# Readout: the projection of tile j ahead of the logits of tile j-2 in the tensor engine's turn

## The chip, the cores and the metric

The kernel runs on one NeuronCore of a Trainium2 chip. The core has five engines that run side by side, each with its own queue of instructions in program order: TensorE (PE, with its weight loads shown apart as PEld), VectorE (DVE), ScalarE (ACT), GpSimd (POOL) and SyncE (SP), which here issues DMAs. They meet at semaphores. The metric is the device time of one execution in microseconds (us), less is better; a figure for a kernel is the median of several runs.

## The reference

One layer of a diffusion backbone over 2048 latent tokens of width 1024, with 256 context tokens ahead of them. Two recurrent mixers (HGRN2 and RWKV-7) run in both directions, their outputs are normed and gated, projected and added to the residual, and a mixture of 64 experts in 8 groups follows, of which each token takes two. What the change touches is the end of the mixer and the routing:

```python
def token_mixer(...):
    ...
    out_l = jnp.concatenate([hgrn2_readout(o_l, g_l, hg_norm_w),
                             rwkv7_readout(y_l, *aux_l, rw_r_k, rw_gn_w, rw_gn_b)], -1) @ w_out
    ...
def hier_moe(h, ...):
    ...
    gl = (t @ w_group + b_group).astype(jnp.float32)
    g_idx = jnp.argmax(gl, -1)
    ...
    el = (t @ w_router).reshape(n_tok, N_GROUPS, EXPERTS_PER_GROUP) + b_router
    ...
    top_v, top_i = lax.top_k(el, TOP_K_INNER)
    ...
def reference(...):
    ...
        x = ln_affine(DN_ALPHA * x + g1 * y, ln1_g[l], ln1_b[l])
        h2 = layer_norm(x) * (1.0 + sc2) + sh2
```

## The kernel before

The program runs six stages one after the other: the two input projections, the scans, the readout, the experts and the combination. All engines meet at a barrier between stages. The change is in the readout (lines 1959 to 2455), which handles the 2048 tokens in 16 tiles of 128.

Each engine runs the same loop of turns, j from -1 to 18 (`readout_turns`, L2340), and in turn j it works on tiles at different depths. The order in a turn is written out by hand for each engine, and nothing but semaphores ties the engines' turns together.

For one tile i the work goes like this. DVE makes the right half of `mix` (turn i-1: `mean`, `variance`, `rw_gate`, L2138 to L2161, signals `mixed`), and POOL the left half (`hg_gate`, L2094, waits for `mixed`, signals `hg_part`). In turn i, PE turns mix into PSUM with eight transposes (`turn_mix`, L2293, all transposes are recorded at L2290), ACT copies them to SBUF as `mixT` (`mix_copy`, L2117), and PE multiplies them with `w_out` (`project`, L2324, matmuls at L2332: 16 in the program, two records each in the trace). In turn i+1 DVE adds the residual (`residual`, L2193, two instructions), takes moments, norms (L2203, L2204, and L2211, L2212, which make `h` and signal `h_ready`). SP stores h. In turn i+2 PE turns h (`turn_h`, L2300), ACT copies it to `hT` (`h_copy`, L2124), and PE makes the 72 router logits of the tile (`logits`, L2306, matmuls at L2314: 8 in the program, 16 records).

Four tiles make a batch b for the routing, which DVE does in four steps spread over four turns: `route_group`, `route_experts`, `route_onehot`, `route_rank`. `routed(j, step)` (L2346) gives the turn: step s of batch b is in turn 4b+5+s, for the last batch in turns 17 and 18. In DVE's turn the routing step stands behind the second moments (up to L2185) and ahead of `rw_gate` and `second_norm`. `pe_ranks` (L2321, L2322) is PE's part of the third step.

The waits around the change are these:

```python
def project(self, pe, i):
    pe.wait_ge(s["mix_copied"], 2 * i + 2)
    wait(pe, s["residual"], i)
...
def logits(self, pe, i):
    pe.wait_ge(s["h_copied"], 2 * i + 2)
    ...
    wait(pe, s["logits_read"], i // BATCH)
...
def h_copy(self, act, i):
    act.wait_ge(s["h_turned"], i + 1)
    wait(act, s["logits_done"], i)
...
def residual(self, dve, i):
    dve.wait_ge(s["projected"], i + 1)
...
def route_group(self, dve, b):
    dve.wait_ge(s["logits_done"], BATCH * (b + 1))
```

`project` and `residual` share one pair of PSUM buffers, so project(j) waits until residual(j-1) has read them. The first instruction of `route_group` behind its wait is L2230, which reads the logits of four tiles from PSUM.

Of the kernel before, what the change touches and what calls it, by code (L numbers as in the profile page):

```python
# [2339 lines left out]
def readout_turns(turn):  # L2340

    for j in range(-1, N_TILES + 3):
        turn(j, j % 2)


def routed(j, step):  # L2346

    for b in range(N_TILES // BATCH):
        last = b == N_TILES // BATCH - 1
        if j == BATCH * b + 5 + (step // 3 if last else step):  # L2350
            return b
    return None


def readout(nc, A, S, K):
    with ExitStack() as ctx:
        m = Mem(nc, ctx, "read")
        r = Readout(nc, m, A, S, K)
        s = r.s
        tile = lambda i: 0 <= i < N_TILES  # L2360

        with nc.Block() as block:
            @block.sync
            def _(sp):
                r.start_loads(sp)

                def turn(j, u):
                    if tile(j + 2) and not (isinstance(j, int) and j < 0):
                        r.load(sp, j + 2, u)
                    if tile(j):  # L2370
                        r.load_x(sp, j)
                    if tile(j - 1):
                        r.store(sp, j - 1)
                readout_turns(turn)
                sp.wait_ge(s["h_stored"], 16 * N_TILES)

            @block.gpsimd
            def _(pool):
                r.op = Order(pool, s["order_pool"])
                nc.gpsimd.memset(r.heps[:], HEAD_EPS).then_inc(s["eps_set"], 1)  # L2380
                nc.gpsimd.memset(r.yeps[:], GN_EPS).then_inc(s["eps_set"], 1)
                pool.wait_ge(s["eps_set"], 2)

                def turn(j, u):
                    if tile(j + 1):
                        r.hg_add(pool, j + 1, 1 - u)
                    if tile(j - 1):
                        r.power(pool, j - 1, 0)
                    if tile(j + 1):
                        r.hg_power(pool, j + 1)  # L2390
                        r.rw_power(pool, j + 1)
                    if tile(j - 1):
                        r.power(pool, j - 1, 1)
                    if tile(j + 1):
                        r.hg_gate(pool, j + 1, 1 - u)
                readout_turns(turn)

            @block.scalar
            def _(act):
                def turn(j, u):  # L2400
                    if tile(j):
                        r.mix_copy(act, j)
                    if tile(j - 2):
                        r.h_copy(act, j - 2)
                    if tile(j + 1):
                        r.hg_squares(act, j + 1, 1 - u)
                        r.y_square(act, j + 1)
                        r.v_scale(act, j + 1, 1 - u)
                        r.hg_scale(act, j + 1, 1 - u)
                    if routed(j, 2) is not None:  # L2410
                        r.exps(act, routed(j, 2))
                readout_turns(turn)

            @block.tensor
            def _(pe):
                def turn(j, u):
                    if tile(j):
                        r.turn_mix(pe, j)
                    if tile(j - 2):
                        r.turn_h(pe, j - 2)  # L2420
                    if routed(j, 3) is not None:
                        r.pe_ranks(pe, routed(j, 3))
                    if tile(j - 2):
                        r.logits(pe, j - 2)
                    if tile(j):
                        r.project(pe, j)
                readout_turns(turn)

            @block.vector
            def _(dve):  # L2430
                r.oa, r.ob, r.oc = (Order(dve, s[f"order_{x}"]) for x in "abc")
                nc.vector.memset(r.run[:], 0.0).then_inc(s["order_start"], 1)
                parts = (r.route_group, r.route_experts, r.route_onehot, r.route_rank)

                def turn(j, u):
                    if tile(j - 1):
                        r.residual(dve, j - 1)
                    if tile(j + 1):
                        r.mean(dve, j + 1, 1 - u)
                    if tile(j - 1):  # L2440
                        r.first_norm(dve, j - 1)
                    if tile(j + 1):
                        r.variance(dve, j + 1, 1 - u)
                    if tile(j - 1):
                        r.moments(j - 1, 1)
                    for step in range(4):
                        if routed(j, step) is not None:
                            parts[step](dve, routed(j, step))
                    if tile(j + 1):
                        r.rw_gate(dve, j + 1, 1 - u)  # L2450
                    if j == -1:
                        r.fold(dve)
                    if tile(j - 1):
                        r.second_norm(dve, j - 1)
                readout_turns(turn)
# [610 lines left out]
```

## Time and profile before

| | |
|---|---|
| median of three runs | 4197.87 us (4196.18 to 4203.44) |
| the profiled execution, whole | 4199.46 us |
| its span, first to last instruction | 4197.8 us |
| PE busy in the span | 3892.4 us, 93% |
| DVE busy in the span | 2049.4 us, 49% |
| ACT, POOL busy in the span | 1174.2 us and 1172.4 us, 28% each |
| the readout | from about 2396 to 2775 us of the span |

Busy time is the time in which an engine executes. An idle time is put down to whatever ended it, so "idle 2.46 <- PE" at an instruction of DVE means that DVE had nothing to do for 2.46 us until PE signalled. The granted clock of TensorE is given as a share of 2.4 GHz; 0.50 is 1.2 GHz. The ends of matmuls are modelled, so consecutive rows of PE can overlap a little.

### The profile page before, as it was taken

The numbers are of one execution on the slowest core, as the hardware profiler recorded it, in microseconds if no ns is written. First come the engines' busy times: TensorE is split into PE (matmuls) and PEld (weight loads), VectorE is DVE, ScalarE is ACT, GpSimd is POOL, SyncE is SP. The second block draws the span as 40 slices with busy tenths as digits, with TensorE's granted clock in tenths as the row PEclk, the third lists the DMA queues.
The fourth block names the chain that finished last, engine by engine and source line by source line (L and its number), as shares of the span: only waits on it lengthen the run. The fifth ranks groups of instructions, "written<-read, shape, count | busy, mean of one in ns | idle before, by whom it ended". The sixth has DMA issues, their size and how long they took to land. (4 is left out here: it accounts for less than half of the span.)

```text
span 4197.8 us, 102804 instructions
## 1 busy us (share of the span) xinstructions
PE 3892.4 (93%) x40204; PEld 2601.7 (62%) x40204; DVE 2049.4 (49%) x3485; ACT 1174.2 (28%) x2889; POOL 1172.4 (28%) x1498
## 2 busy tenths in 40 slices
PE   7999889999996999999999689859999999999988
PEld 5888666666666899999999645443333434343333
DVE  2221277677764776766766489951111111111116
ACT  1111244454543544544554333300000000000000
POOL 0000111101110545555654444433222222222220
PEclk9999899999998999999999889959999999999999
DMA  9821366656655444444444364434668999999986
GB/s 363 211 74 64 104 213 205 206 182 200 211 170 166 136 124 131 131 126 132 129 134 123 108 171 139 130 125 183 258 247 344 394 403 395 400 405 420 420 334 245
DMA packets 318478, 908.16 MB, mean 216 GB/s; under 512 B 67353, under 2 KB 164921, under 8 KB 269361
## 3 DMA queue, kind: packets, MB, share of 16 engines
q1 hardware_dynamic: 261056, 754.99, 51.1%
q0 software_dynamic: 46992, 131.41, 8.5%
q10 hardware_dynamic: 10080, 16.79, 1.1%
q8 instruction: 257, 4.21, 0.4%
q14 instruction: 93, 0.75, 0.1%
HBM read 960.84 MB, written 200.17 MB: 277 GB/s over the span
## 5 line engine op out<-in xcount | busy, mean ns | idle before, releaser
L2804 PE MATMUL exp_gate_up<-exp_w_gate,exp_rows_and_rowsT 128*64 128x512 f32 x1664 | 731.5, 596 | 13.4 <-DMA exp_w_up<-in_moe_w_up_dram 12.2
L2804 PE MATMUL exp_gate_up<-exp_w_up,exp_rows_and_rowsT 128*64 128x512 f32 x1664 | 732.0, 596 | 0.0
L2804 PEld LDWEIGHTS exp_gate_up<-exp_w_gate,exp_rows_and_rowsT 128*64 128x64 f32 x1664 | 227.7, 138 | 482.4 <-issue 482.4
L2755 DVE TENSOR_TENSOR exp_hidden<-exp_hidden,exp_gate_up 64x512 f32<-64x512 f32 x104 | 71.9, 692 | 701.0 <-ACT exp_hidden L2736 701.0
L884 PE MATMUL rwp_product<-rwp_hT,rwp_w_rw 128*128 128x256 f32 x1808 | 393.4, 380 | 12.2 <-DVEq L818 12.2
L1065 PE MATMUL hgp_product<-hgp_hT,const_w_hg 128*128 128x256 f32 x1664 | 379.0, 383 | 8.7 <-DVEq L1046 8.7
L2829 PE MATMUL exp_down<-exp_w_down,exp_hiddenT 128*64 128x512 f32 x1664 | 380.0, 597 | 3.2 <-issue 0.7
L884 PEld LDWEIGHTS rwp_product<-rwp_hT,rwp_w_rw 128*128 128x128 f32 x1808 | 343.9, 191 | 59.2 <-issue 12.6
L1065 PEld LDWEIGHTS hgp_product<-hgp_hT,const_w_hg 128*128 128x128 f32 x1664 | 313.8, 192 | 60.4 <-issue 10.8
L2736 ACT ACTIVATE exp_hidden<-exp_gate_up 64x512 f32<-64x512 f32 x104 | 61.2, 589 | 945.4 <-PE exp_gate_up L2804 945.4
L2713 POOL DMA_INDIRECT s_yb<-exp_out,exp_row_slot x104 | 104.4, 1004 | 571.8 <-PE exp_rows_turned L2789 446.5
L2332 PE MATMUL read_projected<-read_w_out,read_mixT 128*128 128x512 f32 x512 | 236.6, 622 | 8.6 <-DVE read_w_out L2173 7.2
L508 POOL TENSOR_TENSOR hg_scaled_qk<-hg_qkf,hg_exponent 128x256 f32<-128x256 f32 x224 | 199.7, 892 | 151.5 <-ACT hg_exponent L468 123.5
L1062 PE MATMUL hgp_product<-const_w_hg,hgp_hT 128*128 128x512 f32 x544 | 238.6, 594 | 2.4 <-DVEq L1046 2.4
L2829 PEld LDWEIGHTS exp_down<-exp_w_down,exp_hiddenT 128*64 128x64 f32 x1664 | 123.0, 136 | 185.5 <-issue 180.6
L2804 PEld LDWEIGHTS exp_gate_up<-exp_w_up,exp_rows_and_rowsT 128*64 128x64 f32 x1664 | 227.7, 138 | 0.0
L2767 DVE TENSOR_TENSOR exp_out<-exp_down,exp_out_gate 128x512 f32<-128x512 f32 x104 | 71.9, 692 | 305.5 <-PE exp_down L2829 305.5
L1686 PE MATMUL rw_inverse_bank<-rw_inverse_turned,rw_A_rho_beta 64*64 64x64 f32 x5760 | 194.4, 221 | 13.5 <-issue 8.5
L1694 PE MATMUL rw_inverse_bank<-rw_inverse,rw_X 64*64 64x64 f32 x5760 | 193.2, 220 | 3.5 <-ACT rw_X L1747 3.2
L581 DVE TENSOR_TENSOR hg_exponent<-hg_logf_sum 128x512 f32<-128x512 f32 x224 | 196.3, 876 | 0.0
L1686 PEld LDWEIGHTS rw_inverse_bank<-rw_inverse_turned,rw_A_rho_beta 64*64 64x64 f32 x5760 | 180.0, 136 | 23.8 <-issue 19.2
L1694 PEld LDWEIGHTS rw_inverse_bank<-rw_inverse,rw_X 64*64 64x64 f32 x5760 | 178.8, 135 | 13.5 <-issue 8.9
(427 smaller groups left out, 6923.9 us busy)
## 6 DMA issues: line engine op xcount, KB each, us to landing
exp_w_gate<-in_moe_w_gate_dram SPq DMA_DIRECT2D x208, 1024.0 KB
exp_w_up<-in_moe_w_up_dram SPq DMA_DIRECT2D x208, 1024.0 KB
exp_w_down<-in_moe_w_down_dram SPq DMA_DIRECT2D x104, 2048.0 KB
s_rw_in<-prep_operands SPq DMA_DIRECT2D x72, 514.0 KB, 4.0
rw_operands<-s_rw_in SPq DMA_DIRECT2D x72, 514.0 KB, 4.4
hg_qkf<-s_hg_in SPq DMA_DIRECT2D x36, 768.0 KB, 4.7
rw_tokens<-s_rw_tm SPq DMA_DIRECT2D x144, 192.0 KB, 5.0
prep_raw<-s_rw_lat SPq DMA_DIRECT2D x16, 1664.0 KB, 8.0
```

The source lines that it names most:

```text
L508: nc.gpsimd.tensor_tensor(zk, level_views(k, d, l)[1], dk, ALU.mult)
L581: nc.vector.tensor_tensor(v, bv, ref.broadcast_to(bv.shape), ALU.subtract).then_inc(s["diff_ready"], 1)
L884: mm = nc.tensor.matmul(mp[o % 2][:, 0:GROUP], w_in[:, k, c], hT[b][:, k, :], start=(k == 0), stop=(k == KD - 1))
L1062: mm = nc.tensor.matmul(self.mp[o % 4][:], self.hT[b][:, k, j * P:(j + 1) * P], self.w[:, k, c0:c0 + D_HG], start=(k == 0), stop=(k == KD ...
L1065: mm = nc.tensor.matmul(self.mp[o % 4][:, 0:GROUP], self.w[:, k, c0:c0 + P], self.hT[b][:, k, :], start=(k == 0), stop=(k == KD - 1))
L1686: i = nc.tensor.matmul(self.pa[d][q, v, j, :], self.ar[u][d][q, v, j, 0, :], self.rT[d][q, v, j, :], start=True, stop=True)
L1694: i = nc.tensor.matmul(self.pa[d][q, v, j, :], self.x[d][q, v, j, :], self.r[u][d][q, v, j, :], start=True, stop=True)
L2332: mm = self.nc.tensor.matmul(self.py[j][:], self.mT[:, k, :], self.w_out[:, k, j * 512:(j + 1) * 512], start=(k == 0), stop=(k == KD - 1))
L2713: pool.indirect_dma_start(out=S["yb"].rearrange("r (c e) -> (r c) e", c=2), out_offset=bass.IndirectOffsetOnAxis(ap=slot[u][:, 0:1], axis= ...
L2755: nc.vector.tensor_tensor(hid[u][H], hid[u][H], pgu[u][H], ALU.mult).then_inc(s["hid_ready"], 1)
L2804: i = nc.tensor.matmul(pgu[u][q:q + BLK], xT[:, k, r * BLK:(r + 1) * BLK], w[r][:, k, :], start=(k == 0), stop=(k == KD - 1))
L2829: i = nc.tensor.matmul(pd[u][c * 64 + x:c * 64 + x + BLK], hT[u][:, k, x:x + BLK], wd[r][:, k, c * 512:(c + 1) * 512], start=(k == 0), sto ...
```

## The change

In PE's turn of the readout `project(j)` and `logits(j-2)` change places. The waits inside them stay, and nothing is added or removed on any engine.

```diff
                     if routed(j, 3) is not None:
                         r.pe_ranks(pe, routed(j, 3))
+                    if tile(j):
+                        r.project(pe, j)
                     if tile(j - 2):
                         r.logits(pe, j - 2)
-                    if tile(j):
-                        r.project(pe, j)
                 readout_turns(turn)
```

On PE, the stretch of the readout from turn 2 on (each pair of L2290 rows opens a turn: mix of tile j, h of tile j-2), the difference of the two programs:

```order
 L2290 MATMUL read_turned<-const_ident,read_mix 128x128 x8
 L2290 MATMUL read_h_turned<-const_ident,read_h 128x128 x8
+L2332 MATMUL read_projected<-read_w_out,read_mixT 128x512 x16
 L2314 MATMUL read_logits_psum<-read_w_router,read_hT 128x72 x8
-L2332 MATMUL read_projected<-read_w_out,read_mixT 128x512 x16
```

The 16 matmuls of the projection move ahead of the 8 of the logits; turns 2 to 15 all change like this. In turns 0 and 1 there are no logits, and in turns 16 to 18 no projection.

On PE, the turns in which `pe_ranks` runs too (8 and 12), the same difference:

```order
 L2290 MATMUL read_turned<-const_ident,read_mix 128x128 x8
 L2290 MATMUL read_h_turned<-const_ident,read_h 128x128 x8
 L2321 MATMUL read_rank_psum<-read_both,const_earlier_tokens 128x256
 L2322 MATMUL read_rank_psum<-read_counts_before,const_ones 128x256
+L2332 MATMUL read_projected<-read_w_out,read_mixT 128x512 x16
 L2314 MATMUL read_logits_psum<-read_w_router,read_hT 128x72 x8
-L2332 MATMUL read_projected<-read_w_out,read_mixT 128x512 x16
```

The rank matmuls keep their place ahead of both.

On DVE, turn 5 from the end of the second moments (the same in both programs):

```order
L2185 TENSOR_SCALAR read_mean_var<-read_mean_var 128x1
L2230 TENSOR_TENSOR read_logits<-read_logits_psum,read_router_bias 128x288
L2234 TENSOR_REDUCE read_group_max<-read_logits 128x4
...
L2243 TENSOR_REDUCE read_in_group<-read_picked 128x32
L2157 TENSOR_TENSOR read_y_sum<-read_y_sum,read_rw_rstd 128x512
...
L2161 TENSOR_TENSOR read_mix<-read_y_sum,read_rw_g 128x512
L2211 SCALAR_TENSOR_TENSOR read_h<-const_x,read_mean_var,read_scale 128x1024
L2212 SCALAR_TENSOR_TENSOR read_h<-read_h,read_rstd,read_shift 128x1024
L2193 SCALAR_TENSOR_TENSOR const_x<-read_x,read_projected 128x512 x2
```

Nothing moves here; L2230 reads what PE's L2314 of turns 2 to 5 wrote.

## Rows read from the trace of the kernel before

**Rows 1.** Windows view, whole readout: stretch, its us, each engine's busy time, PEclk, DMA.

```profile
core 0: us, PE busy (x) PEld busy (x) DVE busy (x) ACT busy (x) POOL busy (x), PEclk, DMA share, GB/s
2396.00:2775.00 379.00, 306.57 (x1040) 163.94 (x1040) 315.75 (x594) 112.93 (x408) 140.92 (x128) 0.89 0.47 140
```

**Rows 2.** Waits view, 2440 to 2770 us: who waited for whom, total us, times, longest.

```profile
PE read_logits_psum L2314 <- ACT read_hT L2124: 16.8, 16, 1.3
...
DVE const_x L2193 <- PE read_projected L2332: 11.8, 5, 6.2
...
DVE read_logits L2230 <- PE read_logits_psum L2314: 6.9, 1, 6.9
```

**Rows 3.** Timeline of DVE, line L2193, start and us, turns 3 to 16.

```profile
2479.47 1.41 DVE L2193 SCALAR_TENSOR_TENSOR const_x<-read_x,read_projected 128x512 f32<-128x512 f32 x2 [0.19 <-PE read_projected L2332]
...
2499.98 1.41 DVE L2193 SCALAR_TENSOR_TENSOR const_x<-read_x,read_projected 128x512 f32<-128x512 f32 x2 [2.46 <-PE read_projected L2332]
...
2520.49 1.41 DVE L2193 SCALAR_TENSOR_TENSOR const_x<-read_x,read_projected 128x512 f32<-128x512 f32 x2 [2.46 <-PE read_projected L2332]
...
2541.09 1.39 DVE L2193 SCALAR_TENSOR_TENSOR const_x<-read_x,read_projected 128x512 f32<-128x512 f32 x2
...
2561.52 1.41 DVE L2193 SCALAR_TENSOR_TENSOR const_x<-read_x,read_projected 128x512 f32<-128x512 f32 x2 [0.56 <-PE read_projected L2332]
...
2622.47 1.39 DVE L2193 SCALAR_TENSOR_TENSOR const_x<-read_x,read_projected 128x512 f32<-128x512 f32 x2
...
2642.25 1.40 DVE L2193 SCALAR_TENSOR_TENSOR const_x<-read_x,read_projected 128x512 f32<-128x512 f32 x2
...
2722.77 1.40 DVE L2193 SCALAR_TENSOR_TENSOR const_x<-read_x,read_projected 128x512 f32<-128x512 f32 x2
...
2742.68 1.41 DVE L2193 SCALAR_TENSOR_TENSOR const_x<-read_x,read_projected 128x512 f32<-128x512 f32 x2 [6.15 <-PE read_projected L2332]
```

**Rows 4.** Timeline of PE, turn 3, and the projection of turn 10.

```profile
2479.27 1.04 PE L2290 MATMUL read_turned<-const_ident,read_mix 128*128 128x128 f32 x8
2480.14 1.04 PE L2290 MATMUL read_h_turned<-const_ident,read_h 128*128 128x128 f32 x8
2482.46 2.00 PE L2314 MATMUL read_logits_psum<-read_w_router,read_hT 128*128 128x72 f32 x16 [1.28 <-ACT read_hT L2124]
2484.30 15.64 PE L2332 MATMUL read_projected<-read_w_out,read_mixT 128*128 128x512 f32 x32
...
2626.71 13.95 PE L2332 MATMUL read_projected<-read_w_out,read_mixT 128*128 128x512 f32 x32
```

**Rows 5.** Windows view: the first part of projection 3, and turn 17.

```profile
2484.60:2487.90 3.30, 3.30 (x5) 1.35 (x4) 3.07 (x4) 2.81 (x11) 0.42 (x1) 0.50 0.69 150
...
2755.90:2762.80 6.90, 5.66 (x24) 5.06 (x24) 0.01 (x1) 1.08 (x2) 0.00 (x0) 0.50 0.19 76
```

**Rows 6.** Timeline, turn 1: the residual of tile 0 and the projection of tile 1.

```profile
2442.57 1.41 DVE L2193 SCALAR_TENSOR_TENSOR const_x<-read_x,read_projected 128x512 f32<-128x512 f32 x2 [2.35 <-DMA read_x<-in_x_dram]
...
2444.18 15.38 PE L2332 MATMUL read_projected<-read_w_out,read_mixT 128*128 128x512 f32 x32 [1.42 <-DVEq L2194]
```

**Rows 7.** Timeline, turn 10: the transposes of mix on PE and their copy on ACT.

```profile
2621.52 1.09 PE L2290 MATMUL read_turned<-const_ident,read_mix 128*128 128x128 f32 x8 [1.42 <-POOL read_mix L2094]
...
2622.65 1.08 ACT L2117 ACTIVATE read_mixT<-read_turned 128x512 f32<-128x512 f32 x2 [11.43 <-PE read_turned L2290]
```

**Rows 8.** Timeline of PE: projections 0 and 15, transposes and logits of turn 17.

```profile
2422.79 15.83 PE L2332 MATMUL read_projected<-read_w_out,read_mixT 128*128 128x512 f32 x32 [7.21 <-DVE read_w_out L2173]
...
2727.08 15.57 PE L2332 MATMUL read_projected<-read_w_out,read_mixT 128*128 128x512 f32 x32
...
2755.96 1.97 PE L2290 MATMUL read_h_turned<-const_ident,read_h 128*128 128x128 f32 x8 [9.26 <-DVE read_h L2212]
2759.11 3.69 PE L2314 MATMUL read_logits_psum<-read_w_router,read_hT 128*128 128x72 f32 x16 [1.18 <-ACT read_hT L2124]
```

**Rows 9.** Timeline of DVE: the first and the last L2230 (turns 5 and 17).

```profile
2531.78 0.45 DVE L2230 TENSOR_TENSOR read_logits<-read_logits_psum,read_router_bias 128x288 f32<-128x288 f32 x1
...
2762.83 0.46 DVE L2230 TENSOR_TENSOR read_logits<-read_logits_psum,read_router_bias 128x288 f32<-128x288 f32 x1 [6.92 <-PE read_logits_psum L2314]
```

## The prediction

> **What bounds the kernel now.** I read the page first, then the readout's windows, its waits, and its turns one by one on PE, DVE, ACT and POOL. Over the whole span PE is the busiest engine, but the change touches only the readout, 2396 to 2775 us, and there DVE is busy longer (315.75 us of 379) than PE (306.57) [rows 1]. The waits of that stretch [rows 2] say who waits for whom: PE stands 16 times ahead of the logits until ACT has copied hT, 16.8 us in all, and DVE stands only five times for a projection, 11.8 us in all, 6.2 of it once. So the gap on PE comes in every turn, and yet it reaches DVE in few of them.
>
> I write R(j) for the moment at which DVE turn j begins, the first L2193, residual of tile j-1. The rows of L2193 [rows 3] give the lengths of the turns. From R(3) = 2479.47 DVE is ready after 18.05 us (2499.98 less the idle 2.46) and waits 2.46 us for PE; turn 4 is the same. From turn 5 each turn has a step of routing, and DVE needs 20.60 (2520.49 to 2541.09) or 19.87 us (2541.09 to 2561.52, less 0.56). From R(7) = 2561.52 on no row shows idle time until the last projection, 6.15 us ahead of 2742.68. The readout is therefore PE's in turns 3 and 4, DVE's from turn 5 to 15, and the last projection's at the end.
>
> PE's turn 3 [rows 4]: two groups of transposes, 0.87 us from start to start, 1.28 us idle for the copy of hT, logits of 2.00 us, of which the next row overlaps the last 0.16 (2482.46 to 2484.30), and a projection of 15.64 us. In turn 10 the projection takes 13.95 us. In turn 3 the granted clock was 0.50 (1.2 GHz) over its first 3.3 us [rows 5], after transposes, idle time and logits. So a low start costs 1.69 us.
>
> **The change part by part.** The same instructions run on every engine; on PE the 16 matmuls of the logits go behind the 32 of the projection in turns 2 to 15. No DMA is moved in any queue.
>
> *When the projection starts.* project(j) waits for the copies of mixT and for residual(j-1). The second comes later: residual's two instructions began at 2442.57, and project(1), which waited for just this, began at 2444.18 [rows 6], so R + 1.61. The transposes begin at R - 0.95 (2621.52 against R(10) = 2622.47, waiting for POOL), and ACT's copies of mixT end at 2623.73, R + 1.26 [rows 7]. So project(j) runs from R + 1.61 to R + 15.56. Nothing of PE makes DVE wait at R(j+1) then, even in a turn of 18.05 us: four of the five waits, 11.8 - 6.15, go [rows 2, 3]. **Gain 5.67 us.** PE fits into the short turns: 13.79 + 1.84 + at most 2.1 for transposes is 17.7. If the low start came back there, PE's turn would be about 19.4 (15.48 + 1.84 + 0.87 + 0.87 + some 0.35 for ACT and the hand-over), and 2.7 of the gain would go.
>
> *The last projection.* Before, R(16) lies 19.91 us behind R(15) (2722.77 to 2742.68), of which 15.57 us are a projection with a low start [rows 3, 8]. After it can be 1.61 + 13.95 + 0.03 = 15.59, a gain of 4.32. Against it: turn 14 follows a long idle time of PE (below). From a cold start a group of transposes takes 1.97 us (the row after 9.26 us idle) and a projection 15.83 (the row after 7.21 us idle) [rows 8], so project(14) ends between R + 16.9 and R + 18.8, its logits between R + 18.8 and R + 20.7, where the transposes of turn 15 are due at R + 18.85. project(15) is late by 0 to 1.85 us. I take 0.3, near the lower end, because in the row of 15.83 nothing ran ahead of the projection and here 3.9 us of transposes do. **Gain 4.0 us** (2.5 to 4.3; 0.8 if project(15) also starts low).
>
> *The logits, later.* In turn i + 2 PE now gives logits(i) only behind project(i+2): they end at R + 1.61 + 13.95 - 0.16 + 2.00 = R + 17.40, and DVE can follow 0.03 later, as in the row that waits for logits (2759.11 + 3.69 to 2762.83) [rows 8, 9]. For most tiles nobody asks for them that early: h_copy(i+1) on ACT asks a turn later, behind transposes that PE issues behind these logits in any case. But route_group(b) in DVE turn 4b+5 asks for four tiles' logits, the last of which is logits(4b+3), given by PE in that same turn. DVE arrives at L2230 at R + 11.29 (2531.78 against 2520.49) [rows 3, 9], without waiting today. It will wait 17.43 - 11.29 = 6.14 us, in turns 5, 9 and 13. The fourth L2230, in turn 17, has no projection ahead of it and stays. Behind the waiting L2230 in DVE's queue stand the rest of route_group, L2157 to L2161, which make mix(j+1), for which POOL's gate and PE's next transposes wait, and L2211 and L2212, which make h. Nothing of the next turn can run ahead, and turns 6 to 8 and 10 to 12 have no wait for PE on DVE that could pay it back, but the 0.56 already counted. SP's store of h and the loads behind it slide along; those loads are for the tile after next, and no row of these turns waits for them. **Cost 3 x 6.14 = 18.4 us.** Its lower bound is 5.9 each, if residual hands over 0.2 us faster than in [rows 6], its upper 7.8, if these projections start low (1.69 more).
>
> *What the wait leaves behind.* PE ends its logits at R + 17.40 of a stalled turn of 20.60 + 6.14 and has nothing until the transposes at R + 25.8: 8.4 us idle. After 9.26 us of idle time PE ran at a granted clock of 0.50 and took 1.97 us for eight transposes that took 1.04 in turn 3 [rows 4, 5, 8]. The rows also say that turns 6 and 10 hide it: there the projection ends by R + 18.8 and a turn has 19.8 us (2622.47 to 2642.25) [rows 3]; the next projection is late by at most 1.85 and still ends by R + 17.4. Only what turn 14 passes on counts, and that is in the gain above. The Trainium skill, TensorE: Matmul & The Clock Gate, section "Why this matters for your kernels", asks that no idle gaps stand between bursts of matmuls, since idling puts the clock back to its low level; it speaks against a change that makes three such gaps. By it alone, with nothing to hide them, the three turns behind would cost 2 x 0.9 + 1.9 us each, some 11 us more by an estimate from these rows.
>
> *Sum.* 18.4 - 5.67 - 4.0 = +8.7 us; with the favourable ends, 3 x 5.9 - 5.67 - 4.32, it is +7.7. The profiled execution took 4199.46 us, 1.7 of it outside its span of 4197.8; this gives 4208.2. The median of the three runs, 4197.87, is 1.6 lower, and the runs lie between 4196.18 and 4203.44. I add to the profiled time and not to the median: three of the low starts that I take as gone (turns 3, 4 and 15) are in that execution's time, and an execution without them starts lower and gains less, so the time after is the same.
>
> **The rivals.** *Low clock.* The projections of the stalled turns, or those of turns 3 and 4, start low. For it: six projections before did, those of turns 3 to 7 and 15, at 15.57 to 15.64. Against it: logits and transposes now run without the 1.28 us of idle time between, and in turns 8 to 14 a similar pause brought no fall. Price 3 x 1.69 = 5.1 in the stalled turns, to 4213.3; with the 2.7 of the short ones 4216.
>
> *No wait at L2230.* This one ends on the other side. If PE runs so far ahead of DVE that the fourth logits are there when DVE arrives, only the gains are left: 4199.46 - 9.7 = 4189.8. It decides at R + 11.29: project(j) would have to start by R - 4.5. Against it stand the wait for residual(j-1), which DVE does at R itself, and mix(j), which is there only at R - 0.95.
>
> **How the numbers follow.** About 0.2%, 8.4 us, is what a measurement of this kernel can tell from no change; from the median that is 4189.5 and 4206.3. The forecast, 4208, has a chance of 0.74; with a spread between executions like that of the three runs it comes out above 4206.3 a little more often than not (0.42) and otherwise within (0.32). Low clock has 0.20, nearly all above. No wait at L2230 has 0.06, of which 0.04 is faster and 0.02 within. That makes 0.62 slower, 0.34 the same, 0.04 faster. The range, 4201 to 4214, takes in the forecast with its spread and the lesser price of the low clock, and leaves out the other side.
>
> **What would show it.** In the changed trace: L2193 without idle time in turns 3 to 7; L2230 idle three times for PE's logits, near 6.1 us each, in turns 5, 9 and 13, some 18 us more than now in the waits; PE idle some 8 us behind each; project(15) beginning near R + 1.6, and R(16) 15.6 to 17 us behind R(15); the next stage 8 to 10 us later. I am wrong in the main step if L2230 does not wait, in a size if the projections of the stalled turns take 15.6 us, and in the early gain if L2193 still waits in turns 3 and 4.

## The result and the profile after

The changed kernel took 4209.40 us (median of 7 runs, 4207.59 to 4217.87) against 4197.87 (7 runs, 4196.18 to 4203.44). The ratio is 1.0028, with an interval of 1.0019 to 1.0038: slower by about 8 to 16 us, with 4208 forecast and 4201 to 4214 as the range. The profiled execution took 4209.40 us, with a span of 4207.8.

The waits of the readout, of the kernel after, 2440 to 2790 us (who waited for whom, total us, times, longest), against [rows 2]:

```profile
PE read_turned L2290 <- POOL read_mix L2094: 31.3, 7, 8.4
...
DVE read_logits L2230 <- PE read_logits_psum L2314: 24.9, 4, 6.9
...
DVE const_x L2193 <- PE read_projected L2332: 1.9, 1, 1.9
...
PE read_logits_psum L2314 <- ACT read_hT L2124: 1.5, 2, 1.2
```

PE's gap ahead of the logits, 16.8 us in 16 pieces before, is down to 1.5 us in two, and DVE's wait for projections from 11.8 to 1.9. So much for what the change took away. DVE's wait for logits went from 6.9 (one wait) to 24.9 (four): the old one is still there, and three new ones came to 18.0 us. PE waits for mix in pieces of up to 8.4 us.

The same on DVE, kernel after, L2193 and L2230 (start us, duration, what ended the idle time before), against [rows 3, 9]:

```profile
2476.21 1.40 DVE L2193 SCALAR_TENSOR_TENSOR const_x<-read_x,read_projected 128x512 f32<-128x512 f32 x2
2494.17 1.40 DVE L2193 SCALAR_TENSOR_TENSOR const_x<-read_x,read_projected 128x512 f32<-128x512 f32 x2
2512.13 1.39 DVE L2193 SCALAR_TENSOR_TENSOR const_x<-read_x,read_projected 128x512 f32<-128x512 f32 x2
2529.47 0.46 DVE L2230 TENSOR_TENSOR read_logits<-read_logits_psum,read_router_bias 128x288 f32<-128x288 f32 x1 [6.00 <-PE read_logits_psum L2314]
2538.77 1.40 DVE L2193 SCALAR_TENSOR_TENSOR const_x<-read_x,read_projected 128x512 f32<-128x512 f32 x2
...
2731.71 1.39 DVE L2193 SCALAR_TENSOR_TENSOR const_x<-read_x,read_projected 128x512 f32<-128x512 f32 x2
2747.32 1.41 DVE L2193 SCALAR_TENSOR_TENSOR const_x<-read_x,read_projected 128x512 f32<-128x512 f32 x2 [1.85 <-PE read_projected L2332]
```

Turns 3 and 4 are 17.96 us long without a wait (20.51 before). Turn 5, 2512.13 to 2538.77, is 26.64 us long (20.60 before), and L2230 stands in it for 6.00 us. Turns 9 and 13 show the same 6.00 and 26.65. R(16) lies 15.61 us behind R(15) (19.91 before).

PE's turns 5 and 6 and the projections of turns 14 and 15, kernel after, against [rows 4, 7, 8]:

```profile
2513.72 13.97 PE L2332 MATMUL read_projected<-read_w_out,read_mixT 128*128 128x512 f32 x32 [0.37 <-DVEq L2194]
2527.53 1.90 PE L2314 MATMUL read_logits_psum<-read_w_router,read_hT 128*128 128x72 f32 x16
2537.82 1.97 PE L2290 MATMUL read_turned<-const_ident,read_mix 128*128 128x128 f32 x8 [8.39 <-POOL read_mix L2094]
2539.58 1.92 PE L2290 MATMUL read_h_turned<-const_ident,read_h 128*128 128x128 f32 x8
2541.29 14.50 PE L2332 MATMUL read_projected<-read_w_out,read_mixT 128*128 128x512 f32 x32
...
2714.44 14.96 PE L2332 MATMUL read_projected<-read_w_out,read_mixT 128*128 128x512 f32 x32
...
2733.31 13.97 PE L2332 MATMUL read_projected<-read_w_out,read_mixT 128*128 128x512 f32 x32 [0.37 <-DVEq L2194]
```

project(5) begins at R + 1.59 and the logits behind it end at 2529.43; L2230 follows 0.04 us later. Then PE has nothing for 8.39 us, and the transposes behind it take 1.97 us, as after the 9.26 us of [rows 8]. The windows view of this place (columns as in [rows 1]) has the clock:

```profile
2537.80:2541.40 3.60, 3.58 (x17) 3.58 (x18) 3.42 (x5) 1.09 (x2) 2.18 (x1) 0.50 0.47 151
2541.60:2544.90 3.30, 3.30 (x8) 1.32 (x8) 2.96 (x8) 2.70 (x11) 1.91 (x3) 0.87 1.00 283
```

A granted clock of 0.50 (1.2 GHz) over the transposes, 0.87 on average over the first part of the projection, which so took 14.50 us in place of 13.97.

From R(1) to R(16) the readout takes 307.74 us, against 300.11 before: +7.63, made up as follows.

| part | before | after | difference |
|---|---|---|---|
| turns 5, 9, 13 | 20.60, 20.56, 20.57 | 26.64, 26.65, 26.65 | +18.2 |
| turns 2 to 4 | 18.23, 20.51, 20.51 | 17.96 each | -5.4 |
| turns 6 and 7 | 20.43, 20.52 | 19.80, 20.28 | -0.9 |
| turn 15 | 19.91 | 15.61 | -4.3 |

The spans of the two profiled executions are 10.0 us apart (4197.8 and 4207.8): 7.6 us of it is this, 5.4 us lies behind R(16), and the stretch ahead of R(1) is 3.0 us shorter.

### The profile page after: what moved, and what is told of

Its sections match the earlier page's. It is cut to its first block and busy times, and to the rows that moved or that the text cites. A ratio compares the mean times of both kernels' runs of the same rounds, so it can differ in the third digit from the quotient of the medians.

```text
span 4207.8 us, 102804 instructions
## 1 busy us (share of the span) xinstructions
PE 3887.1 (92%) x40204; PEld 2605.8 (62%) x40204; DVE 2048.6 (49%) x3485; ACT 1175.4 (28%) x2889; POOL 1174.2 (28%) x1498
## 5 line engine op out<-in xcount | busy, mean ns | idle before, releaser
L1065 PEld LDWEIGHTS hgp_product<-hgp_hT,const_w_hg 128*128 128x128 f32 x1664 | 313.8, 192 | 60.4 <-issue 10.8
L1686 PE MATMUL rw_inverse_bank<-rw_inverse_turned,rw_A_rho_beta 64*64 64x64 f32 x5760 | 194.4, 221 | 13.6 <-issue 8.3
```

Source lines behind the costliest of these rows:

```text
L1065: mm = nc.tensor.matmul(self.mp[o % 4][:, 0:GROUP], self.w[:, k, c0:c0 + P], self.hT[b][:, k, :], start=(k == 0), stop=(k == KD - 1))
L1686: i = nc.tensor.matmul(self.pa[d][q, v, j, :], self.ar[u][d][q, v, j, 0, :], self.rT[d][q, v, j, :], start=True, stop=True)
```

## The experiments

The times below are medians, each with the kernel before on the same chip. The sums R(1) to R(16) come from one profile each, and the stretch ahead of R(1), which no edit touches, ends anywhere from 2431.9 to 2446.5 us, so single executions say less than the sums.

| kernel | R(1) to R(16), us | median, us | before, us | ratio (interval) |
|---|---|---|---|---|
| before, again | 294.15 | 4189.60 (one run) | 4195.87 | |
| after, again | 307.80 | 4215.39 (one run) | 4195.87 | |
| routing a turn later | 288.87 | 4186.99 | 4198.85 | 0.9973 (0.9962 to 0.9983) |
| new order but in 5, 9, 13 | 291.16 | 4190.56 | 4198.85 | 0.9980 (0.9970 to 0.9989) |
| new order in 5, 9, 13 alone | 321.39 | 4220.78 | 4198.85 | 1.0056 (1.0041 to 1.0070) |
| new order in 2 to 4 alone | 292.15 | 4193.94 | 4198.85 | 0.9986 (0.9977 to 0.9995) |
| new order in 15 alone | 291.54 | 4191.17 | 4195.87 | 0.9988 (0.9978 to 0.9997) |
| routing at the turn's end | 301.69 | 4199.86 | 4197.97 | 1.0010 (0.9998 to 1.0023) |
| routing ahead of the variance | 321.86 | 4222.31 | 4197.97 | 1.0062 (1.0045 to 1.0079) |

The theory: the loss is the wait of L2230 for logits that are given later in the same turn, three times; the rest of the change gains. The rival: the loss comes from elsewhere, from PE's low clock behind its idle time, or from the stage behind the readout. In that stage the profile after has 6.0 us of idle time ahead of PE's L2507 that no other engine ended ("issue") and that the profile of before has not.

### The same two kernels once more

No edit.

> The kernel before, unchanged, for a second profiled execution. If the low starts of projections are not tied to the program, some turns of 2 to 4 and 15 will differ from the first (turns 3 and 4 of 18.8 instead of 20.5 us, turn 15 of 18.2 instead of 19.9), and R(1) to R(16) is 295 to 300 us. If the idle time of 6 us at PE's L2507 in the next stage is not tied to the change, it may show here too; if it is, it will not.

> The changed kernel, unchanged, for a second profiled execution. The three waits of 6.0 us at L2230 and turns 2 to 4 of 17.96 us come again, since no projection there starts at the low clock; R(1) to R(16) is 307.7 us within 1.

The kernel after repeats itself: three waits at L2230 of 6.00, 5.99 and 5.99 us, the last turn 15.61. The kernel before does not. Its L2193 of turns 3 to 5 and 16, second profile:

```profile
2471.77 1.41 DVE L2193 SCALAR_TENSOR_TENSOR const_x<-read_x,read_projected 128x512 f32<-128x512 f32 x2 [0.18 <-PE read_projected L2332]
2490.59 1.41 DVE L2193 SCALAR_TENSOR_TENSOR const_x<-read_x,read_projected 128x512 f32<-128x512 f32 x2 [0.77 <-PE read_projected L2332]
2509.40 1.41 DVE L2193 SCALAR_TENSOR_TENSOR const_x<-read_x,read_projected 128x512 f32<-128x512 f32 x2 [0.77 <-PE read_projected L2332]
...
2729.02 1.41 DVE L2193 SCALAR_TENSOR_TENSOR const_x<-read_x,read_projected 128x512 f32<-128x512 f32 x2 [4.46 <-PE read_projected L2332]
```

The waits of 2.46, 2.46 and 6.15 in [rows 3] are 0.77, 0.77 and 4.46 here, each 1.69 less: the projections of turns 3 to 7 and 15 took 13.95 us in this execution. Of turns 2 to 15 only that of turn 11 started low (15.64 us), and DVE didn't wait for it. The readout, 294.15 us, is a little below the 295 to 300 that I had put. The change so costs 7.6 us of readout against one execution and 13.6 (307.74 - 294.15) against another, and the measured 11.5 lies between. Also, that idle time at L2507 is 5.9 us in this profile of the kernel before too, and 5.7 to 7.3 in the second profile of after and in those of all the kernels below: it isn't the change's.

### Routing a turn later

PE's new order stays whole, but route_group asks a turn after the last of its logits was given. The function that says at which turn a batch's steps run:

```diff
         last = b == N_TILES // BATCH - 1
-        if j == BATCH * b + 5 + (step // 3 if last else step):
+        at = (17, 17, 17, 18) if last else (14, 15, 15, 16) if b == 2 else tuple(BATCH * b + 6 + s for s in range(4))
+        if j == at[step]:
```

> The changed order on PE, with the routing steps of batches 0 and 1 one turn later (route_group in turns 6 and 10) and those of batch 2 in turns 14, 15, 15, 16. Theory of the wait (DVE loses 3 x 6.0 us at L2230 because the fourth tile's logits now end behind the projection of the same turn): L2230 waits only in turn 17, the distance from R(1) to R(16), 307.7 us in the changed kernel and 300.1 before, falls by 18.0 for the waits and up to 1.9 more, as the steps now in turn 15 fill its idle time: 288 to 290 us. The time is then 4188 to 4191 us, ratio to before 0.9975 to 0.9985. Rival (the loss comes with the new order on PE itself, by what follows in the next stage, where the changed kernel's profiled execution had 6.0 us of idle time at PE's L2507): the readout shrinks as above, but the 6 us at L2507 stay, and the time is about 4195, ratio 0.999 or above.

L2230 of turns 6, 10 and 14 has no idle time; only that of turn 17 waits. DVE, turns 5 and 6, and the last L2193:

```profile
2524.75 1.39 DVE L2193 SCALAR_TENSOR_TENSOR const_x<-read_x,read_projected 128x512 f32<-128x512 f32 x2
2536.01 0.45 DVE L2230 TENSOR_TENSOR read_logits<-read_logits_psum,read_router_bias 128x288 f32<-128x288 f32 x1
2545.31 1.40 DVE L2193 SCALAR_TENSOR_TENSOR const_x<-read_x,read_projected 128x512 f32<-128x512 f32 x2
...
2723.10 1.41 DVE L2193 SCALAR_TENSOR_TENSOR const_x<-read_x,read_projected 128x512 f32<-128x512 f32 x2 [0.66 <-PE read_projected L2332]
```

The turn that holds L2230 takes 20.56 us again, and the short turns stay at 17.95 to 17.97, now four of them. The last is 16.73: project(15) took 15.06 us there, a partly low start in the new order (granted clock 0.66 over its first 3.3 us). With the three waits gone the kernel is 11.9 us faster than before instead of 11.5 slower, a little more than I had put (4188 to 4191). Of the 18.9 us between the two readouts (307.74 and 288.87) 18.0 are the waits; the other 0.9 fits the two routing steps that now share turn 15, where DVE had to wait for the projection anyway. Routing a turn later in the old order was not run, so what that move brings by itself is not shown. The kernel is the fastest of this study: what the reorder takes away was worth having, and the routing only asked a turn too early for it.

### The change in some turns only

PE's turn takes the new order where a list says so, and the old one elsewhere; the list is the only thing that differs among four kernels (this one: all turns from 2 but 5, 9 and 13; the diff is against the kernel after):

```diff
-                    if tile(j):
+                    ahead = j in (2, 3, 4, 6, 7, 8, 10, 11, 12, 14, 15)
+                    if tile(j) and ahead:
                         r.project(pe, j)
                     if tile(j - 2):
                         r.logits(pe, j - 2)
+                    if tile(j) and not ahead:
+                        r.project(pe, j)
```

> The changed order, except in turns 5, 9 and 13, where the logits stand ahead of the projection as before. Theory of the wait: in these turns project starts near R + 4.2 and ends near R + 18.2, inside DVE's 20.6 us, and L2230 does not wait; R(1) to R(16) is 307.7 - 18.0 = 289.7 us, time 4190 to 4192 us, ratio 0.998. Rival (the next stage): the readout as here, but 6 us stay at L2507, time about 4197, ratio 1.000.

No wait at L2230 in turns 5, 9 and 13, and a kernel faster than before by 0.2%. Two of the three projections in the old order, those of turns 5 and 9, started low (15.64 us each); only the second made DVE wait, 0.33 us. project(15), in the new order, took 15.06 us, and the last L2193 waited 2.97. Turn 9 so became 20.98 us and turn 15 16.73, which are the 1.5 us by which the readout lies above the expected 289.7.

The opposite, `ahead = j in (5, 9, 13)`:

> The order of before, with the projection ahead of the logits in turns 5, 9 and 13 alone. Theory of the wait: the three waits without the gains. 6.0 us in turns 9 and 13, 6 to 8.2 in turn 5, where PE may still start its projection at the low clock; the 0.56 us of turn 7 may go. R(1) to R(16) is 300.1 + 17.5 to 20.2 = 317.6 to 320.3 us, time 4215 to 4218 us, ratio 1.0042 to 1.0048. Rival (gains and losses are spread over all turns): about a fifth of the changed kernel's +7.6, 302 us.

The three waits came as expected, 6.42, 5.99 and 5.99 us, but the kernel is slower than I said, 4220.78 and 321.39 us against 4215 to 4218 and 317.6 to 320.3. The missing piece stands in the turns behind. PE, turn 6, then turn 10, of this kernel:

```profile
2533.03 1.97 PE L2290 MATMUL read_turned<-const_ident,read_mix 128*128 128x128 f32 x8 [8.39 <-POOL read_mix L2094]
2534.80 1.91 PE L2290 MATMUL read_h_turned<-const_ident,read_h 128*128 128x128 f32 x8
2537.88 3.69 PE L2314 MATMUL read_logits_psum<-read_w_router,read_hT 128*128 128x72 f32 x16 [1.17 <-ACT read_hT L2124]
2541.36 15.87 PE L2332 MATMUL read_projected<-read_w_out,read_mixT 128*128 128x512 f32 x32
...
2628.20 2.00 PE L2314 MATMUL read_logits_psum<-read_w_router,read_hT 128*128 128x72 f32 x16 [1.17 <-ACT read_hT L2124]
2630.05 13.95 PE L2332 MATMUL read_projected<-read_w_out,read_mixT 128*128 128x512 f32 x32
```

And DVE at the ends of turns 6 and 14:

```profile
2557.27 1.41 DVE L2193 SCALAR_TENSOR_TENSOR const_x<-read_x,read_projected 128x512 f32<-128x512 f32 x2 [3.42 <-PE read_projected L2332]
...
2734.47 1.41 DVE L2193 SCALAR_TENSOR_TENSOR const_x<-read_x,read_projected 128x512 f32<-128x512 f32 x2 [3.69 <-PE read_projected L2332]
```

Behind 8.39 us without work PE runs low, and with the old order the wait for hT, the slow logits and the slow start of the projection come one after the other: logits 3.69, projection 15.87 (16.16 in turn 14). DVE then waits 3.42 and 3.69 us. In turn 10 the clock had risen by the logits (1.00 granted over them, 0.50 in turns 6 and 14), which took 2.00 and the projection 13.95 us, and nothing waited. In the kernel after, only the transposes stand between the same idle time and the projection of turn 6, which begins at R + 2.52 and, with its 14.50 us, ends at R + 17.02, inside a turn of 19.80. So the low clock can cost 3.5 to 3.8 us in a turn, and it is the new order in turns 6, 10 and 14 that keeps it from costing. These costs are larger than the excess over my sum, because this execution had no low starts in turns 3, 4 and 15 of the old order, which the 300.1 us that I started from had.

The two gains by themselves, `ahead = j in (2, 3, 4)` and `ahead = j in (15,)`:

> The order of before, with the projection ahead of the logits in turns 2, 3 and 4 alone. Theory: the waits of DVE at L2193 in turns 3, 4 and 5 (0.19, 2.46, 2.46) go, and no wait at L2230 comes: R(1) to R(16) is 300.1 - 5.1 to 5.9 = 294.2 to 295.0 us, time 4192 to 4193 us, ratio 0.9987. If a start at the low clock comes back in these turns, 2.7 less: 297.

> The order of before, with the projection ahead of the logits in turn 15 alone. Theory: project(15) starts near R(15) + 1.6 and R(16) lies 15.6 us behind R(15), or 17.3 if it starts at the low clock; before it was 19.9 with a low start and 18.2 without one. Gain 2.6 to 4.3 us, time 4194 to 4197 us, ratio 0.9990 to 0.9994.

Turns 2 to 4 came to 17.96, 17.95 and 17.96; the last turn alone to 15.61 (18.23 in the second profile of before, where project(15) did not start low either, so 2.62 of gain there; 4.30 against the first). Both kernels are faster by about 0.1%, as expected in sign. The first came to 4193.94 where I had put 4192 to 4193, and its readout, 292.15, below the 294.2 to 295.0; the second came below the 4194 to 4197 that I had put.

### Where in DVE's turn the routing stands

If the wait is the distance between DVE's arrival at L2230 and PE's logits at R + 17.4, its place in the turn sets it. Two kernels move the routing's loop in DVE's turn, to its end and to ahead of the variance (first diff; the second moves the same three lines up past the variance and the moments):

```diff
                         r.moments(j - 1, 1)
-                    for step in range(4):
-                        if routed(j, step) is not None:
-                            parts[step](dve, routed(j, step))
                     if tile(j + 1):
                         r.rw_gate(dve, j + 1, 1 - u)
...
                         r.second_norm(dve, j - 1)
+                    for step in range(4):
+                        if routed(j, step) is not None:
+                            parts[step](dve, routed(j, step))
```

> The changed order on PE; in DVE's turn the routing steps stand earlier, ahead of variance and the second moments. Theory of the wait: the logits come at R + 17.3 as before, DVE comes to L2230 at R + 8.3 and waits 9.0 us instead of 6.0, and the 3.2 us of work that stood ahead of it, with 0.4 of waiting for rw_rstd, come behind: each of turns 5, 9 and 13 is 30.2 us instead of 26.65, and seven more turns bear the 0.4. R(1) to R(16) is 307.7 + 10.7 + 2.9 = 321.3 us, time 4219 to 4226 us, ratio 1.005 to 1.007. Rival (the wait only shifts DVE's work, which has slack): 307.7 us stays.

> The changed order on PE; in DVE's turn the routing steps stand at the end, behind second_norm, instead of ahead of rw_gate. Theory of the wait: the fourth logits end at R + 17.3 and DVE now comes to L2230 only at R + 18.0, so it waits in turn 17 alone and the 18.0 us go; the wait for POOL's rw_rstd ahead of L2157, 0.41 us, is no longer covered by routing and comes in ten turns more, 4.1 us. R(1) to R(16) is 307.7 - 18.0 + 4.1 = 293.8 us, time 4190 to 4196 us, ratio 0.9980 to 0.9995. Rival (the order of the matmuls on PE is slow in itself): 307.7 us stays.

Ahead of the variance the waits are 9.14, 9.14 and 9.15 us and the stalled turns 30.17 to 30.19: the wait follows DVE's arrival, as expected. PE still gives the logits at nearly the same place, L2230 starting at R + 17.43 (2528.69 against 2511.26; R + 17.34 in the kernel after):

```profile
2528.69 0.46 DVE L2230 TENSOR_TENSOR read_logits<-read_logits_psum,read_router_bias 128x288 f32<-128x288 f32 x1 [9.14 <-PE read_logits_psum L2314]
```

At the turn's end the waits are gone, as expected, yet the kernel is no faster than before, where I had put 4190 to 4196 and 293.8 us. Its turns 5 to 14 take 213.5 us, those of the kernel with the new order in turns 2 to 4 alone 201.4. What became longer, DVE and POOL in turns 5, 6 and 7 of this kernel:

```profile
2524.47 0.19 DVE L2234 TENSOR_REDUCE read_group_max<-read_logits 128x4 f32<-128x32 f32 x1
2524.69 0.56 DVE L2236 TENSOR_TENSOR read_group_exp<-read_logits,read_group_max 128x32 f32<-128x32 f32 x1
...
2545.64 1.04 DVE L2222 TENSOR_TENSOR read_first_at<-read_in_group,read_top 128x32 f32<-128x32 f32 x1
...
2566.55 1.23 DVE L2258 TENSOR_SCALAR read_group_base<-read_group_down 128x4 f32<-128x4 f32 x1
```

```profile
2522.95 2.26 POOL L2061 TENSOR_TENSOR read_hg_o<-read_hg_o 128x512 f32<-128x512 f32 x1
...
2544.39 2.24 POOL L2061 TENSOR_TENSOR read_hg_o<-read_hg_o 128x512 f32<-128x512 f32 x1
...
2565.51 2.25 POOL L2061 TENSOR_TENSOR read_hg_o<-read_hg_o 128x512 f32<-128x512 f32 x1
```

The three long DVE rows end at 2525.25, 2546.68 and 2567.78, and POOL's pass beside each at 2525.21, 2546.63 and 2567.76. In the kernel after, where none of these rows begins inside POOL's L2061, L2236 and L2222 take 0.19 us, and L2258 0.16. Nine such rows, with L2276 of turn 8 (1.02 in place of 0.16), come to 6.7 us: 3 x 0.37 + 2 x 0.85 + 2 x 1.07 + 2 x 0.86. Some 4.1 us more is L2157, which now follows the second moments at once and waits 0.41 us in each of these ten turns for POOL's rw_rstd; in the other kernel it waits in turns 1 to 4 alone, and the routing covers the rest. That is 10.8 of the 12.1 us; the remainder is small gaps of DVE's own, such as 0.22 us at the ends of turns 7 and 11 and 0.34 us more ahead of L2203 in turn 13. So the last place in the turn falls into POOL's pass L2061, and the routing isn't free there.

## Why the prediction was right

*The logits, later.* The main step, 3 x 6.14 = 18.4 us, measured 18.2. Each wait is 6.00: the logits run without the idle time for hT ahead of them and take 1.90 us where I took 2.00, project(j) begins at R + 1.59 and not 1.61, and DVE comes at R + 11.34 and not 11.29. The three experiments that move DVE's arrival or PE's order took the wait away, and the fourth, ahead of the variance, made it longer by 3.14 us as DVE came 3.05 earlier (R + 8.29 against R + 11.34); that it is this wait is shown.

*The short turns.* 5.67 put, 6.2 measured against the first profile. The waits went as said, and the turns became 17.96 where I had 18.05 or so; turn 7 also shrank by 0.24. No projection of turns 2 to 5 took more than 14.00 us, so the low start did not come back there.

*The last projection.* 4.0 put with bounds of 2.5 to 4.3; 4.30 measured. The 0.3 for a late project(15) was not needed: project(14), which took 14.96 us and not 15.8, ended early enough.

*What the wait leaves behind.* 8.39 us idle for 8.4 forecast, a clock of 0.50, transposes of 1.97 and 1.92 us, and no wait in turns 6, 10 and 14. The estimate beside it, some 11 us with nothing to hide the low clock, did not come true in this kernel. The Trainium skill, TensorE: Matmul & The Clock Gate, section "Why this matters for your kernels", warns of just such gaps; the trace agrees that the clock falls (0.50 behind 8.39 us), and the kernel with the new order in turns 5, 9 and 13 alone shows the price where the order behind the gap is the old one, 3.5 and 3.8 us (23.28 and 23.56 against 19.80), in two turns of three.

*The sum.* +8.7 put. The readout's terms came to +7.6 against the profile that I worked from, and the measured difference of medians is 11.5. The step that was too simple is the one on the median: I took the low starts of turns 3, 4 and 15 to be in that execution's time and the time after to be the same whatever they did. The readout after is indeed the same (307.74 and 307.80), but that of the kernel before varies by 6.0 us (300.11 and 294.15) with them, so a difference read from one execution is off by up to that. Taking the profiled time as the base gave 4208.2. Its nearness to 4209.4 is in part luck: the stretches ahead of R(1) and behind R(16), which the sum takes as unchanged, differed by -3.0 and +5.4 us between the two profiled executions.

*The rivals.* No wait at L2230 fell in the first row. Low clock fell as well: 13.97 us for the projections of the stalled turns.

*What stays open.* Why the same program in the old order starts some projections low in one execution and others in the next was not settled. Of turns 2 to 15 they were those of turns 3 to 7 and 15 in the first profile of before, that of turn 11 alone in the second, those of turns 5 and 9 in the kernel that keeps the old order there, that of turn 7 in the kernels with the new order in turns 2 to 4 alone and in turns 5, 9 and 13 alone, and none in the kernel with the new order in turn 15 alone. In the new order the projections of turns 2 to 4 took 13.97 to 14.00 us in all seven profiles in which they stood in it, and that of turn 15 took 13.97 in five profiles and 15.06 in two (the routing a turn later, and the old order in 5, 9 and 13). That is a hint and no proof, for the new order has low starts as well: with the routing at the turn's end the projections of turns 6, 8, 10, 12 and 14 took 15.65 to 16.90 us. In that kernel PE comes early and stands idle right ahead of the projection until residual is done, in turn 6 for 3.86 us:

```profile
2529.07 16.90 PE L2332 MATMUL read_projected<-read_w_out,read_mixT 128*128 128x512 f32 x32 [3.86 <-DVEq L2194]
```

The granted clock was 0.50 over the first 3.3 us of this row. All five ended inside their turns, and DVE waited for none.

## What to carry to other kernels

When work is moved ahead on an engine that runs in order, look for the reader of what it was moved past, and compare that reader's arrival with the new time of the data: here three of the fourteen turns that were reordered decided the sign. If the reader can ask one turn later, move it along with the change; that turned +0.28% into -0.27%. A place in the queue that looks free for small instructions must also be free of its neighbour's passes.

## What the runs showed of the hardware that I had not expected

**DVE's instructions stop for POOL's wide passes.** Instructions of 0.16 to 0.19 us took 0.56 to 1.23 us when they began inside POOL's pass L2061 (128x512), and ended 0.02 to 0.05 us behind it. The row just ahead of the first, the reduction L2234, began inside the same pass and took its usual 0.19 us, and so did the L2230 ahead of that, which reads PSUM (0.45). The Trainium skill, SBUF — State Buffer, section "SBUF: two separate sides", has DVE and GpSimd share a pair of ports as an exclusive lock for the whole instruction, which a DVE instruction needs if it runs in a two-port mode, or if it has two inputs in SBUF and the instruction of GpSimd reads SBUF. These rows agree: the rows with two inputs (L2236, L2222, L2276) were held, the reduction was not. Whether the TENSOR_SCALAR row ran in such a mode no run here shows. Other rows do not agree: in the kernel after, L2222 and L2258 began inside POOL's L2087 (128x8, 1.64 us), with 0.25 and 0.46 us of it to go, and took their usual 0.19 and 0.16 us. By that section L2222, with its two inputs, would have had to wait; the measurement decides. So here it is POOL's 128x512 passes that hold DVE, and not every instruction of POOL.

The costliest such row stands in every kernel of this study. L2212, which has two inputs in SBUF, begins inside POOL's L2094 in fourteen turns and takes 2.17 us there; in the last two it has no such pass beside it and takes 1.28. That is some 12 us of DVE's time in one readout, as much as the 11.5 us that the change costs; what of it could be won back no run here shows. Its line in the kernel after (busy us, mean ns of one, idle before):

```profile
L2212 DVE SCALAR_TENSOR_TENSOR read_h<-read_h,read_rstd,read_shift 128x1024 f32<-128x1024 f32 x16 | 32.9, 2059 | 0.6
```

**The same low clock costs or not by what stands first behind the gap.** After 8.39 us of idle time the order transposes, projection, logits lost up to 1.0 us of PE's time in the projection (13.90 to 14.96 against 13.97) and none of DVE's, in all six gaps of the two profiles of after. The order transposes, logits, projection lost 3.6 us on PE in turn 6 (3.69 - 2.00 and 15.87 - 13.95) and 3.42 on DVE, and 3.9 and 3.69 in turn 14; in turn 10 it lost none. So the order behind the gap set whether the low clock reached DVE in these gaps; how long the clock stayed low differed from gap to gap.
